# Hybrid dilated-attention encoder on eight cores: twelve halo tiles transposed by DMA instead of by TensorE

## The reference

```
h    = rmsnorm(x) * norm_g
proj = h @ w_in                       # 1024 -> 9216: q, k, v, z_a, hc, gb, gc, z_b, g
attn = three head groups (window, dilation) = (128,1), (512,4), (2048,16), 8 heads of 64 each,
       64 keys per side at stride d, ALiBi bias; groups combined by their softmax denominators
a    = (silu(z_a) * attn) @ w_attn_out
c    = (silu(z_b) * gb * conv3(gc * hc)) @ w_conv_out
y    = rmsnorm(x + (sigmoid(g_a)*a + sigmoid(g_c)*c) @ w_o) * final_g
```

## Time and profile before

| | |
|---|---|
| median of 3 runs | 1474.95 us (1474.83 to 1476.91) |
| profiled execution | 1475.44 us |
| span of its slowest core (7) | 1473.9 us |
| spans of the eight cores | 1467.9 to 1473.9 us |
| busy: TensorE | 1455.8 us (99%) |
| VectorE, ScalarE, GpSimd | 885.7, 661.0, 175.4 us |
| DMA | 139.21 MB, mean 94 GB/s |

### The profile page before, as it was taken

The page is one execution under the profiler, slowest core; times in us unless marked ns, Lnnn a source line. Parts: engine busy times, 40 slices in busy tenths (PEclk is TensorE's granted clock), DMA queues, the critical chain, the costliest instruction groups (busy, mean ns, idle before and its releaser), DMA issues.

```text
span 1473.9 us, 30536 instructions; the slowest of 8 cores (1467.9 to 1473.9 us)
## 1 busy us (share of the span) xinstructions
PE 1455.8 (99%) x13213; PEld 846.3 (57%) x13213; DVE 885.7 (60%) x1191; ACT 661.0 (45%) x1010; POOL 175.4 (12%) x320
## 2 busy tenths in 40 slices
PE   8998999999999999999999999999999999999998
PEld 5656765665655544444455767877776444444443
DVE  4776473473573896554466458394765967433357
ACT  4576455555455422443232556565655311222234
POOL 3431000000010010232011101000100100000000
PEclk9999999999999999999999999999999999999999
DMA  9974234153154141999495524425342522222158
GB/s 227 207 141 98 59 75 72 20 92 54 20 101 77 29 74 22 173 147 174 83 299 153 117 61 66 93 38 73 68 67 30 87 51 42 31 34 43 22 183 273
DMA packets 114218, 139.21 MB, mean 94 GB/s; under 512 B 73586, under 2 KB 73618, under 8 KB 114084
## 3 DMA queue, kind: packets, MB, share of 16 engines
q0 software_dynamic: 27728, 54.65, 23.2%
q1 hardware_dynamic: 86356, 82.61, 23.2%
HBM read 145.97 MB, written 23.66 MB: 115 GB/s over the span
## 4 chain that ended last, share of the span: by engine, by line
PE 95%; DMA 3%; DVE 1%; SPq 0%; ACT 0%; issue 0%; DVEq 0%; ACTq 0%; POOLq 0%
PE ps L456 86%; PE ps L468 8%; DMA Y<-xw 2%; DMA wbf<-wblk 1%; PE ps L483 1%; SPq L487 0%; DMA hnT<-Y 0%; DVE Y L420 0%; ACT Y L407 0%; DVE hnT L444 0%; DVE Y L411 0%; DVE Y L444 0%; DVEq L1385 0%; ACT Y L443 0%; ACT hnT L443 0%
## 5 line engine op out<-in xcount | busy, mean ns | idle before, releaser
L456 PE MATMUL ps<-hnT,wbf 128*128 128x512 bf16 (+4 forms) x5648 | 1023.6, 338 | 3.3 <-DMA wbf<-wblk 2.4
L456 PEld LDWEIGHTS ps<-hnT,wbf 128*128 128x128 bf16 x5648 | 522.3, 98 | 443.9 <-DMA wbf<-wblk 2.9
L407 ACT ACTIVATE Y<-ps 128x1024 bf16<-128x1024 f32 (+1 forms) x292 | 240.9, 873 | 194.6 <-PE ps L456 146.0
L443 ACT ACTIVATE Y<-ps 128x512 bf16<-128x512 f32 (+2 forms) x307 | 183.1, 597 | 268.0 <-PE ps L456 246.9
L411 DVE TENSOR_TENSOR Y<-ps,Y 128x512 f32<-128x512 f32 (+1 forms) x196 | 125.6, 673 | 205.0 <-PE ps L468 170.5
L420 DVE SCALAR_TENSOR_TENSOR Y<-Y,ps 128x512 f32<-128x512 f32 x192 | 130.6, 683 | 171.4 <-PE ps L456 146.1
L487 POOL DMA_DIRECT2D wbf<-wblk x160 | 87.7, 549 | 959.0 <-PE ps L456 945.1
L407 ACT ACTIVATE Y<-ps,cf 128x512 f32<-128x512 f32 x128 | 87.6, 688 | 215.7 <-PE ps L456 200.5
L411 DVE TENSOR_TENSOR Y<-Y,et 128x1024 bf16<-128x1024 bf16 x192 | 129.6, 685 | 18.3 <-ACT Y L407 14.0
L407 ACT ACTIVATE Y<-Y 128x1024 bf16<-128x1024 f32 (+3 forms) x83 | 86.0, 1036 | 120.4 <-DVE Y L420 85.8
L468 PEld LDWEIGHTS ps<-Y 64*128 64x128 bf16 x4640 | 114.4, 94 | 31.5 <-issue 26.5
(11 more groups left out here) (48 smaller groups left out, 410.8 us busy)
## 6 DMA issues: line engine op xcount, KB each, us to landing
wbf<-wblk POOLq DMA_DIRECT2D x160, 256.0 KB, 5.0
Y<-xw SPq DMA_DIRECT2D x56, 512.0 KB, 8.2
Y<-xw SPq DMA_DIRECT2D x48, 256.0 KB, 6.8
y<-Y POOLq DMA_DIRECT2D x16, 512.0 KB, 4.3
y<-Y SPq DMA_DIRECT2D x15, 512.0 KB, 6.6
Y<-wblk POOLq DMA_DIRECT2D x16, 256.0 KB, 8.2
et<-etab SPq DMA_DIRECT2D x8, 384.0 KB, 3.9
cv<-Y SPq DMA_DIRECT2D x4, 768.0 KB, 6.3
```

The source lines that it names most:

```text
L407: R.add("act", [lambda e: e.activation(out=out.a, in_=in_.a, func=func, scale=scale, **kw)], c_act(in_.n) + (0.2 if accum is not None else ...
L443: return e.activation(out=out.a, in_=in_.a, func=AF.Copy)
L456: fns = [(lambda e, m=m: e.matmul(m[0].a, lhsT=m[1].a, rhs=m[2].a, start=m[3], stop=m[4])) for m in mms]
```

## The change

Four things together. The twelve far tiles get no PSUM bank: they are transposed as a whole by one DMA transpose each into one of four staging buffers hst of 2 KB per partition, at 104 to 112 KB. The sixteen copies that sort the residues apart read the staging buffer instead of PSUM. Their sixteen loads go through GpSimd's queue, with the landing of 2.6 us in the plan (kind "h"). And each chunk's tiles stand one step sooner in the program. In the planner a DMA transpose planned before 140 us is moved behind the modelled end of SP's last plain transfer plus 1.5 us.

```diff
@@ schedule
+            if t0 < 140 and o.dma is not None and o.dma[0] == "t":
+                t0 = max(t0, held)
...
+                if n == "sp" and o.dma[0] != "t":
+                    held = done_at + 1.5
@@ buffers
+        hst = [yb(104 + 2 * i, 2048, BF16) for i in range(4)]
@@ ln_tile
-                d = dma("sp", o.a, bass.AP(xw, ...
+                d = dma("pool" if kind == "h" else "sp", o.a, bass.AP(xw, ...
@@ ln_span
-            ln_tile(loads, dsts, xt0, xn0, gb0, jk0, bank)
+            if bank is not None:
+                return ln_tile(loads, dsts, xt0, xn0, gb0, jk0, bank)
+            st = oldest(hst)
+            ln_tile(loads, [(st, 0, 128, 0, 128)], xt0, xn0, gb0, jk0, None, kind="h")
+            for hcol, hd, pcol, pd in dsts:
+                copy(hnT.ap(hcol, [[WIN, 8]] + hd), st.ap(pcol, [[128, 8]] + pd))
@@ halo
-                        ln_span(c, i0s, n, next_bank())
+                        ln_span(c, i0s, n, None)
-        halos = {(0, 3): halo(0), (1, 0): halo(1), (1, 1): halo(2), (1, 2): halo(3)}
+        halos = {(0, 2): halo(0), (0, 3): halo(1), (1, 0): halo(2), (1, 1): halo(3)}
```

More of the change, by code:

```diff
@@ L180, in schedule @@
         order = []
+        held = 0.0
         def offer(o):
@@ L633, in ln_tile @@
                 o = xt.cols(0, 1024, p0, np_)
-                d = dma("sp", o.a, bass.AP(xw, row0 * D, [[st * D, n] for st, n in dims] + [[1, D]]), list(after),
+                d = dma("pool" if kind == "h" else "sp", o.a, bass.AP(xw, row0 * D, [[st * D, n] for st, n in dims] + [[1, D]]), list(after),
                         [o if k == 0 else parts[k]], 1.7 * np_ / 128, kind)
```

## The result

The changed kernel takes 1490.05 us (median) against 1474.89 for the kernel before: 1.0% slower, ratio 1.010 with the interval 1.0087 to 1.0114. The forecast was 1466, the range 1461 to 1475. In some launches, one of these four among them, the cores of one die run at a lower clock and the time is longer; they are left out of every ratio, and of the medians from here on, by which the changed kernel has 1489.9.

What follows compares the result with a forecast made beforehand. TensorE, 99% busy with a hole at 120 to 140 us, was taken as the bound. Core 1: 1471.0 - 5.7 (transposes) - 2.6 (hole) = 1462.7, plus 2.0 new waits, plus 1.5 outside the span: 1466 us; range 1461 to 1475.

Steps and rivals of the forecast that it cites:

- Added on SP: 12 DMA transposes: Halo tiles on SP: 1.3 us issue plus 4.5 to land each, worst 8.3, hidden by the earlier start.
- the 17 us of cover: From 97.67 us to the keys at 114.83 that need the first tiles; called twice the worst 8.3 us.
- Loads moved to GpSimd ... both covered above: Sixteen halo loads on GpSimd: landing 8.2 us, 3.2 gain or loss per load, covered; nothing charged.
- rival A: Hole at 120 to 140 us stays or moves, only 5.7 us gained: 1469.3 to 1471; 0.16 together with D.
- Planner's hold ... -2 to +2 us, taken as 0: Planned transposes pushed behind SP's loads; said to change only the order of the start.
- Freed by it: xn released when transposes land, loads of tiles 8 to 12 before 105 us; gain 0 to 6.4 (core 7), 2.6 (core 1).
- The worth of the hole: TensorE's hole at 120 to 140 us, idle plus low clock: 6.4 us on core 7, 2.6 on core 1.
- 96 transposes left TensorE: Twelve halo tiles of eight transposes removed from TensorE, 99% busy: 5.7 us gained.
- The copies: Sixteen copies on ScalarE or VectorE, now from SBUF: no change taken, at most -8 to +5 us in sum.
- The earlier step: Halo tiles start one step sooner, from 97.67 us, to hide the DMA transposes' 5.8 us to the staging buffer.
- C: Rival, units 0 and 1: late transposes make staging copies block ScalarE and VectorE, 5.4 us a wait, about 1480; chance 0.13.

Runs made afterwards that it cites:

- e1: Changed kernel with the sixteen halo loads back on SP's queue: 1476.8 us, ratio 1.0014 to the kernel before.
- e13: Changed kernel with halo loads on SP's queue, the 2.5 us landing pad given back and no planner hold: 1472.4 us, ratio 0.9981.
- e14: Changed kernel with the 2.5 us landing pad given back and no planner hold, loads still on GpSimd's queue: 1482.0 us, ratio 1.0047.
- e15: e13 with 3 us more of planned landing for the twelve DMA transposes: 1465.4 us, ratio 0.9937.
- e17: e15 with the sixteen halo loads on GpSimd's queue: 1479.7 us, ratio 1.0049.
- e7: Kernel before with its sixteen halo loads on GpSimd's queue, without their 2.5 us landing pad: 1481.5 us, ratio 1.0051.
- e10: Kernel before with only the 2.5 us landing pad taken from the sixteen halo loads, which stay on SP's queue: 1481.5 us, ratio 1.0049.
- e9: e7 with the 2.5 us landing pad given back to the halo loads: 1472.9 us, ratio 0.999.
- e11: Changed kernel with the 2.5 us landing pad given back to the halo loads: 1484.8 us, ratio 1.0073.
- e2: Changed kernel without the planner's hold of transposes before 140 us: 1485.5 us, ratio 1.0073.
- e6: Changed kernel with halo loads on SP's queue and no planner hold: 1475.2 us, ratio 1.0006.
- e18: e15 with 6 us more of planned landing for the transposes in place of 3: 1479.7 us, ratio 1.0036.

## Why the prediction was wrong

*The step that failed: "Added on SP: 12 DMA transposes", with its price of 4.5 us to land and "worst 1.3 + 7.0 = 8.3".* The rows under it were of transposes with other neighbours: the four own ones had loads on their own queue, the small ones weights. The change puts 128 rows of 4 KB at a time on the other queue, at the very time at which the transposes run. Measured: up to 29.4 us, and the 17 us of cover that I called twice the worst case were not enough. The price of the queue beside DMA transposes, with the plan that comes with it, is 13.1 us (e1), 9.6 (e13 and e14), some 16 (e15 and e17). Beside TensorE transposes it is 0.0 (e7 and e10). Only the pairing costs, and I had priced the two parts each by itself.

What makes it slow is shown only in part. In most stretches in which transposes run beside GpSimd's packets, the DMA engines are full at a low rate, and full at a high one with transposes nearly alone. The last line is a stretch in which both ran and the rate was high. Core 1 of the changed kernel:

```profile
104.00:108.00 4.00, 4.00 (x62) 2.27 (x60) 1.84 (x3) 2.49 (x5) 0.79 (x2) 1.00 1.09 219
...
120.00:124.00 4.00, 2.33 (x52) 2.11 (x46) 0.00 (x0) 0.00 (x0) 0.95 (x1) 1.00 1.30 81
...
150.00:154.00 4.00, 3.33 (x37) 2.39 (x38) 3.90 (x7) 2.22 (x5) 3.06 (x4) 1.00 1.03 211
```

With transposes nearly alone it is 219 GB/s at a share of 1.09, with both 81 at 1.30, and then 211 at 1.03 though a halo load of 512 KB ran beside. Company alone does not make a stretch slow. Nor does it take GpSimd's company: on core 3 of e15, with no load and no weight beside the transposes, 100 to 104 us has 96 GB/s at a share of 1.34, and 22 packets begun within 0.1 us there all take 2.4 to 2.5 us. The Trainium skill, DMA: Bandwidth & Descriptors (Queues, rings and completion order), says that each DMA engine goes round the queues it has work for and empties a whole packet, typically 9 to 17 descriptors, from one before it turns to the next. The trace agrees in part: 5% of the 256-byte packets with company took about one 4 KB packet's time, but the median took 18 ns with company and without, and more of the time went into stalls of many packets at once. By the same page (Rules for kernel authors) a transpose next to ordinary DMAs needs nothing. That stands beside rules on corrupted data and hangs; it says nothing of the time, which here was 9.6 to 16 us longer.

*"Loads moved to GpSimd ... both covered above"*: wrong only beside the transposes, where the loads landed after 14 to 16 us in place of the 8.2 plus 3.2 that I allowed. The rule of the Trainium skill, SBUF — State Buffer (SBUF: two separate sides), that GpSimd can't write descriptors while VectorE holds the ports they share, was not what decided: beside TensorE transposes, and with the pad, GpSimd's loads ran at 1472.9 (e9).

*The pad*, unpriced: kind "h" took 2.5 us of planned landing from loads that land 8.2 after issue in the median. My text noted that landings are planned too short and used it for rival A alone. It costs 7.3 us at TensorE transposes (e10) and 4 to 5 in the changed kernel (e11). The missing step was to follow the new kind into schedule().

*"Planner's hold ... -2 to +2 us, taken as 0"*: by the medians 4.5 us (changed and e2), 2.8 with the pad (e11 and e14), 1.7 on SP (e1 and e6), each pair with intervals that touch or overlap. If it is real, the term was too small, with the loss inside its bounds in one pair of three.

*"Freed by it"*, by which the loads of tiles 8 to 12 "should then go out before 105": they did not. Core 1 issued its last halo load at 149.0 us. xn is freed when a transpose lands, and that was later than TensorE used to take. The worth of the hole was too high as well: priced at 2.6 to 6.4 us, it gave 1.3 us of the launch where it closed (e9).

*What was right:* 96 transposes left TensorE, 145 matmuls of L489 of 241 remain. That they are worth 5.7 us no run shows by itself. e15 has 1465.4, near the forecast's 1466, but that is in part luck: it is another kernel than the one forecast, with the loads on SP's queue, more planned landing for loads and transposes, and no hold; and 3 us of planned landing less or more make it 7 or 14 us slower (e13, e18). The copies: 0.69 us on VectorE and 1.14 on ScalarE, no term of the sum, as assumed. The earlier step cost nothing.

*The rivals:* C named the main mechanism, head-of-line waits on the staging copies, decided by landings, and A's sign came with it, ScalarE waiting for loads: of TensorE's two long waits on core 1, 7.1 us were behind a copy and 6.7 behind a load, at a clock of 0.70 to 0.84. C's price was 5.4 us a wait with two or three waits, and TensorE waited 10.9 + 7.1 us on ScalarE. Landings of 7 us were too kind by a factor of four, so 1480 was 10 short. It had 0.13, which was too little once "beside loads of another queue" was seen to have no row.

## What to carry to other kernels

Try DMA transposes and large plain loads on one queue first: here, with DMA transposes, the queue of the loads and the plan that came with it were worth 9.6 to 16 us, with TensorE transposes nothing. Keeping the two apart in time was not tried. When a change gives a transfer a new kind, follow the kind into the planner; 2.5 us less of planned landing cost 7 us without touching the transfer. And a planner makes neighbours of its own: a change of one number in it moved this kernel by 14 us (e15 and e18), so an effect needs more than one pair. A price from rows holds for the neighbours that those rows had; where the change brings a new neighbour, take the price as unknown on the upper side.

## What the runs showed of the hardware that was not expected

The copies from the staging buffer, groups by form in the changed kernel (us in all, mean ns), against the earlier trace rows:

```profile
L449 ACT ACTIVATE hnT<-Y 128x1024 bf16<-128x1024 bf16 x4 | 4.5, 1136 | 4.0 <-DMA Y<-Y 4.0
L450 DVE COPY hnT<-Y 128x1024 bf16<-128x1024 bf16 x4 | 2.8, 694 | 17.3 <-DMA Y<-Y 17.3
```

With the source in SBUF in place of PSUM, VectorE is faster (0.69 us in place of 0.89 in the mean) and ScalarE slower (1.14 in place of 1.02), with a source stride of four elements on either.
